# Attention in a two-layer encoder: GpSimd scales the probabilities of one head in four, VectorE those of three

## What is computed

```
s = einsum('bnqkgd,bnskd->bnkgqs', q, kb) * 64 ** -0.5        # 4 groups k, 4 heads g in each
s = where(mask, s + bias, -1e30)                              # band of 128 keys to either side
p = softmax(concatenate([s, sink_col], -1), -1)[..., :-1]     # the sink only adds to the sum
o = einsum('bnkgqs,bnskd->bnqkgd', p, vb)
return o.reshape(...) @ w_o
```

## Time and profile before

| | us |
|---|---|
| median of 3 runs | 1587.93 |
| lowest, highest | 1586.76, 1589.08 |
| the profiled execution | 1584.55 |
| its span in the trace | 1582.7 |
| attention's iterations, in the trace | about 918 to 1005 |
| of them, VectorE without a gap | 939.42 to 996.64 |

### The profile page before, as it was taken

How to read it: one execution, slowest core, us unless ns; L and a number is a source line. 1 busy time by engine, 2 the same in 40 slices (tenths; PEclk the granted TensorE clock), 3 DMA queues, 4 the chain that set the end, 5 groups by cost and what they waited for, 6 DMA issues and landing times. The chain is left out here.

```text
span 1582.7 us, 18640 instructions
## 1 busy us (share of the span) xinstructions
PE 1388.3 (88%) x6901; PEld 640.5 (40%) x6901; DVE 529.7 (33%) x1248; ACT 244.0 (15%) x522; POOL 194.4 (12%) x362
## 2 busy tenths in 40 slices
PE   7999999999988888887889978899997887888786
PEld 4544574553333332332334456455332332333232
DVE  6999985251110111111141159335111111011115
ACT  3211121120000000000020047212100000000002
POOL 5200000011111111111000000001121111111100
PEclk9999999999999999999999989999999999999999
DMA  8314436279999999999995100537999999999996
GB/s 251 119 58 94 56 121 266 93 287 385 402 426 427 427 426 427 426 427 426 427 367 194 54 1 2 213 123 302 369 419 427 426 426 426 428 426 428 425 429 257
DMA packets 74021, 479.23 MB, mean 303 GB/s; under 512 B 16152, under 2 KB 23064, under 8 KB 49392
## 3 DMA queue, kind: packets, MB, share of 16 engines
q1 hardware_dynamic: 61392, 454.36, 71.1%
q0 software_dynamic: 11152, 19.27, 3.4%
q10 hardware_dynamic: 1424, 4.89, 0.8%
HBM read 468.01 MB, written 26.74 MB: 313 GB/s over the span
## 5 line engine op out<-in xcount | busy, mean ns | idle before, releaser
L700 PE MATMUL psum<-ring,work 128*64 128x512 f32 x992 | 475.1, 635 | 89.2 <-DMA ring<-in_moe_w_up 89.2
L701 PE MATMUL psum<-ring,work 128*64 128x512 f32 x992 | 475.7, 636 | 0.0
L700 PEld LDWEIGHTS psum<-ring,work 128*64 128x64 f32 x992 | 140.1, 146 | 397.5 <-issue 310.5
L713 PE MATMUL psum<-ring,work 128*64 128x512 f32 x992 | 226.5, 598 | 40.1 <-DVE work L886 39.8
L883 DVE TENSOR_TENSOR work<-work,psum 64x512 f32<-64x512 f32 x64 | 44.2, 690 | 557.4 <-ACT work L840 557.3
L840 ACT ACTIVATE work<-psum 64x512 f32<-64x512 f32 x64 | 37.8, 590 | 800.0 <-PE psum L701 800.0
L701 PEld LDWEIGHTS psum<-ring,work 128*64 128x64 f32 x992 | 140.2, 146 | 2.0
L713 PEld LDWEIGHTS psum<-ring,work 128*64 128x64 f32 x992 | 67.3, 136 | 157.5 <-issue 132.6
L889 DVE COPY work<-psum 128x512 f32<-128x512 f32 x60 | 41.4, 691 | 231.5 <-PE psum L713 231.5
L1793 PE MATMUL psum<-ring,hT 128*128 128x512 f32 x256 | 113.5, 600 | 0.0
L1086 POOL DMA_INDIRECT work<-h_dram,ints x64 | 66.8, 1043 | 56.9 <-POOL ints L1079 53.1
(11 more groups left out here) (382 smaller groups left out, 1406.9 us busy)
## 6 DMA issues: line engine op xcount, KB each, us to landing
ring<-in_moe_w_gate SPq DMA_DIRECT2D x62, 2048.0 KB, 16.9
ring<-in_moe_w_up SPq DMA_DIRECT2D x62, 2048.0 KB, 21.5
ring<-in_moe_w_down SPq DMA_DIRECT2D x62, 2048.0 KB, 21.9
ring<-in_hyb_w_in SPq DMA_DIRECT2D x5, 2048.0 KB, 8.9
work<-y_dram SPq DMA_DIRECT2D x8, 1024.0 KB, 9.4
ring<-in_swa_w_qkv SPq DMA_DIRECT2D x3, 2048.0 KB, 17.8
x_sb<-in_x SPq DMA_DIRECT2D x8, 512.0 KB, 6.3
y_dram<-x_sb SPq DMA_DIRECT2D x1, 4096.0 KB, 18.5
```

What stands on the lines that cost most here:

```text
L700: nc.tensor.matmul(bank[2 + b][0:BLK, :], x, g[:, c, :], start=c == 0, stop=c == KC - 1)
L701: i = nc.tensor.matmul(bank[2 + b][BLK:P, :], x, u[:, c, :], start=c == 0, stop=c == KC - 1)
L713: i = nc.tensor.matmul(bank[6 + b][BLK * hf:BLK * (hf + 1), :], HTE[b][:, c, :], d[:, c, hf * HALF:(hf + 1) * HALF], start=c == 0, stop=c ...
```

## The change

`scale(it)` keeps three of its four multiplications (heads 0 to 2). The reciprocal now raises `probs_scaled`, and so does the third multiplication: the semaphore counts two for each iteration. GpSimd gets a function `pool_scale`, in its queue between the router's transfers and `gain(4)`: for each iteration it waits for the reciprocal and multiplies head 3. TensorE's `probs(it)` waits for the third multiplication and for GpSimd's step (semaphore `pool_steps`, `pool_own`).

```
+        last_head = []
+
+        def pool_scale(pool, Q):
+
+            for it in range(len(ITS)):
+                lo, hi, _ = keys(ITS[it][0])
+                w = P * (hi - lo)
+                st = 16 * (it % 4) + AT0
+                pool.wait_ge(s_sc.s, 2 * it + 1)
+                p = SBF[it % 4][:, 3 * BAND:3 * BAND + w]
+                Q(nc.gpsimd.tensor_scalar(p, p, WK[:, st + 15:st + 16], None, ALU.mult))
+                last_head.append(pool_own.n)
...
-                pe.wait_ge(s_sc.s, it + 1)
+                pe.wait_ge(s_sc.s, 2 * it + 2)
+                pe.wait_ge(pool_own.s, last_head[it])
...
-                V(tv.reciprocal(rc, den))
+                V(tv.reciprocal(rc, den), s_sc)
                 V.sync()
-                for k in range(4):
+                for k in range(3):
                     p = SBF[it % 4][:, BAND * k:BAND * k + w]
-                    V(tv.tensor_scalar(p, p, rc[:, k:k + 1], None, ALU.mult), s_sc if k == 3 else None)
+                    V(tv.tensor_scalar(p, p, rc[:, k:k + 1], None, ALU.mult), s_sc if k == 2 else None)
...
             router_loads(1)
+            pool_scale(pool, Q)
             gain(4)
```

## The result

The changed kernel takes **1594.7 us** (median of 10 runs, 1590.7 to 1597.4) against 1587.5 us of the kernel before (10 runs on the same occasions, 1584.6 to 1592.9): ratio 1.0040, 95% interval 1.0026 to 1.0055. The medians are 7.2 us apart, and the ratio is 6.4 us (4.1 to 8.7) of 1587.5: slower, where 1587.4, 0.5 us faster, was forecast. The profiled execution took 1597.37 us, its span is 1595.5 us.

A forecast was written before the change was run, and what follows sets the result against it. VectorE in attention was taken as the bound. Eight iterations of 0.28 - 0.33 and five of 0.25 - 0.26 gave -0.5 us, so 1587.9 became 1587.4 us; range 1584.0 to 1598.5 us.

The forecast's parts named there:

- The bound: Attention: VectorE, without a gap, sets the 5.03 us spacing at 384 keys; changes reach the end nearly one to one.
- What is removed: One VectorE multiplication an iteration, 0.33 us at 384 columns, 0.26 at 256; 3.9 us over the gapless iterations.
- What TensorE lets through: Attention's circle through TensorE's scores: at most 0.26 us an iteration comes off at either size; ceiling 3.4 us.
- GpSimd's own price: GpSimd's multiplication of head 3: 1.13 us for 384 columns, 0.88 for 256, hidden except 0 to 0.5 us at iteration 0.
- The cover of 3.6 us: Time from the reciprocal's end (962.94) to TensorE's transposes (966.54), within which GpSimd's step was to stay hidden.
- What the two engines do to each other: GpSimd's step beside VectorE's three multiplications: one hold-up of VectorE, 0.28 us for 384 columns, 0.25 for 256.
- The step of 536 columns: Layer 0 GpSimd step, 2.272 us: it cost one VectorE product of two SBUF inputs 0.31 us, the next nothing.
- rival A with a second hold-up: GpSimd holds VectorE up twice an iteration, again when it writes: 3.5 us more, 1590.9 us; chance 0.15.
- the single hold-up: Rival A's main case: one hold-up an iteration, gain and loss cancel, 1587.4 us; chance 0.38.
- Rival B: VectorE stands still for GpSimd's whole instruction: 9.5 us slower, 1597.4, or 1603 by the upper price; chance 0.24.
- Rival C: No collision: GpSimd waits until VectorE's third multiplication is done; full ceiling of 3.4 us, 1584.5 us; chance 0.20.
- The median: Whole program: the runs' median lies 3.4 us above the profiled execution, so 1587.9 - 0.5 = 1587.4 us.

The follow-up runs named there:

- experiment 2: Against the kernel before: ScalarE, not VectorE, scales head 3, and GpSimd does nothing in attention; 1586.68 us, ratio 0.9980.
- experiment 3: Changed kernel, VectorE scaling all four heads again, GpSimd working on unread scratch: full multiplication 1596.64 us, write-only memset 1588.7 us, multiplication of 128 columns 1593.4 us.
- experiment 6: Kernel before plus one VectorE scratch multiplication (384 columns, 64 at 256 keys) ahead of the reciprocal, GpSimd given nothing; 1591.97 us, ratio 1.0018.
- experiment 1: Changed kernel, with GpSimd's step waiting for VectorE's third multiplication instead of the reciprocal; 1588.55 us, ratio 0.9997 against the kernel before.

## Why the prediction was wrong, step by step

- **The bound.** Right. VectorE sets the spacing, and what attention gains or loses reaches the end: 4 us in attention and 5.6 in all between the two executions without half clock in a router, and experiments 2, 3 and 6 go the same way. It holds for the iterations of 384 keys; at 256 keys VectorE has gaps as soon as it is quicker (0.44 us in experiment 1, 0.81 in experiment 2).
- **What is removed.** Right: 0.33 and 0.26 us; with GpSimd or ScalarE out of the way the three multiplications last 0.99 (956.38 - 955.39).
- **What TensorE lets through.** Right in kind, wrong in both its sizes. At 384 keys 0.32 us came off (spacing 4.71, forecast 4.77); at 256 keys next to nothing (12.6 and 13.0 us for three spacings in experiments 1 and 2, 12.8 before). The statement that those iterations give all their 0.26 had no row behind it. Attention gave 2.1 us with ScalarE and not 3.4.
- **GpSimd's own price.** 1.24 and 0.92 us away from the multiplications (experiment 1), 1.47 and 1.08 beside them: inside the bounds of 1.13 to 1.66 and 0.88 to 1.14, and the lower end that was taken was a tenth short. The cover of 3.6 us hid it in the changed kernel; in iteration 0 the transposes started right behind VectorE's third multiplication, which ended after GpSimd's step. In experiment 1 TensorE did wait for it there, 0.9 us, more than the 0 to 0.5 that the forecast had.
- **What the two engines do to each other. This is the step that failed.** One hold-up of 0.28 (0.25) us was taken, from the earlier trace rows. There were two, of 0.33 (0.21): 0.67 and 0.42 us in an iteration. In the sum, 8 x (0.67 - 0.33) + 5 x (0.42 - 0.26) = 2.7 + 0.8 = 3.5 us where -0.5 stood; attention measured 3.8. The size of one hold-up was near; the count was wrong. The weak place is what the count was taken from. The step of 536 columns had two long neighbours, at 50.41 and 51.44, and only the first was held; but they are products of two SBUF inputs, and the forecast itself said that the multiplication differs from those. It let the difference go into the bounds and not into the count. Why the one is held once and the other twice no run shows. That was the rival A with a second hold-up: spacing 5.25 forecast, 5.36 measured, reciprocal to `evac_first` 1.76 forecast, 1.88 measured. It had a chance of 0.15, the single hold-up 0.38. Of the signs of failure that were named, a multiplication over 1 us or three undisturbed ones, neither came: the longest lasts 0.75 us, and a second hold-up wasn't among them.
- **Rival B,** VectorE still for the whole GpSimd instruction (spacing 5.8, the Trainium skill's page "SBUF — State Buffer", section "Who interferes with whom"), did not come: 0.67 us lost for an instruction of 1.47. The section's rule that the engine that comes second is blocked for the whole instruction is not what this trace shows. Its other half, that only VectorE and GpSimd wait for each other there while ScalarE has its own ports, agrees with experiment 2.
- **Rival C** did not come by itself, since GpSimd starts 0.06 us behind VectorE; experiment 1 made it, and it gave 1.7 us of attention, none of it visible in the median.
- **The median.** 4 us of the 7 are attention's. Of the others 1.5 us are between the two executions without half clock in a router (5.6 against 4.0) and have no cause shown. What is left is of the size of the half-clock stretches, which both kernels have, but that it comes from them is not shown. The forecast had no term for them and took the spread of three runs, 2.3 us, for that of the kernel, which is 10 us over 83 executions. That 1594.7 lies inside the range is luck: the range reached so far because of rival B, which didn't come, and the mechanism that did come was priced at 1590.9.

## What to carry to other kernels

Before work goes to GpSimd beside a VectorE instruction from SBUF to SBUF, price the meeting by the columns that GpSimd reads and writes, not by one neighbour's row: here it cost VectorE twice what the removed instruction had cost. Start such a step where VectorE reads PSUM (here that took the loss away and gained nothing that the median shows), or give it to ScalarE, which held none of VectorE's multiplications up here and made the faster kernel. Where the effect is under half a per cent, read several profiled executions of the same kernel before a stretch of one is taken for the kernel's.

## What was not expected of the hardware

- A GpSimd step holds VectorE's multiplications by its columns: 0.14, 0.42, 0.66 us for 128, 256, 384 columns read and written, 0.24 us for 384 columns only written. For 128 columns the loss is the same beside multiplications of 384 and of 256 columns. GpSimd pays too: 1.47 us instead of 1.24.
- Beside the same GpSimd step, VectorE's copy from PSUM and its bias step lose nothing (0.69 and 0.61 us), and beside ScalarE's multiplication (0.62 us) VectorE's three lose nothing.
- The granted clock fell to 0.50 for about 10 us in a router of layer 0 or 1 in six of the eight profiled executions of the two kernels, and cost about 4 us each time, with the same instructions in the router in all eight. One of 7 us at about 257 to 264 us, ahead of attention, made 2.8 of the 4.1 us by which the changed kernel's first profiled execution was late at its first reciprocal.
